# Peer weights of the first group loaded ahead, cache pages as four-key rows, and a new order inside a page group

## What is computed

```
xn = rmsnorm(x); q, c, kr, u_pool, gates = projections(xn @ w_in)
attn = prompt_attention(q, c, kr)                      # prompt: causal, 8 heads
# sample tokens: online softmax over 32 cached pages of 128 keys each, found by a page table
def page_step(carry, phys):
    m, l, acc = carry
    c_pg = ckv_pages[phys]; k_pg = mla_keys(c_pg, kr_pages[phys], p)
    s = einsum('bqhd,bthd->bhqt', q, k_pg) * SCALE
    return online_update(m, l, acc, s, c_pg)           # new maximum, exp, corrected sums
h = x + merge(attn, pool_mix(u_pool), gates) @ w_out
# PEER: per token and head, product keys pick 16 of 16384 experts
q = xn2 @ peer_w_q; s = q @ peer_keys; top 16 of 128 on each side, top 16 of the 256 sums
y = h + sum_e softmax_e * gelu(xn2 . peer_u[e]) * peer_v[e]
```

## Time and profile before

| | us |
|---|---|
| median of 3 runs | 3991.52 (3970.24 to 3993.34) |
| the profiled execution | 3977.99 |
| its span in the trace | 3976.2 |
| group 0 up to its scores | 0 to 292 |
| its scores, until the first expert dot | 292 to 416 |
| experts with groups 1 and 2 | 416 to 1930 |
| experts with the pages | 1930 to 3210 |
| experts with the sample layer, and the rest of the experts | 3210 to 3976 |

### The profile page before, as it was taken

One profiled execution on the slowest core, in us unless ns is written; L12 is line 12 of the kernel. 1 busy time (PEld: TensorE's weight loads), 2 busy tenths in 40 slices (PEclk: granted clock), 3 DMA queues, 4 the chain that ended last, 5 costly groups with the idle time before them and its releaser, 6 DMA issues.

```text
span 3976.2 us, 44748 instructions
## 1 busy us (share of the span) xinstructions
PE 3064.3 (77%) x13299; PEld 1596.3 (40%) x13299; DVE 2684.1 (68%) x6876; ACT 957.7 (24%) x1893; POOL 2394.3 (60%) x2196
## 2 busy tenths in 40 slices
PE   8896888996787888876688888888888866663345
PEld 5665435443442544333344444444444434230001
DVE  2312987665578866666788888888878875656653
ACT  2200123111023320120245444443454411100000
POOL 0000565765676566675766676676667676677776
PEclk9798988997998889998899999899989976666668
DMA  4445798999999989999999999899989999999999
GB/s 132 101 154 186 265 372 326 412 408 373 379 401 388 339 338 411 403 402 373 376 370 331 360 376 358 319 386 362 369 331 365 363 402 414 379 397 383 379 396 376
DMA packets 432834, 1387.34 MB, mean 349 GB/s; under 512 B 60553, under 2 KB 118890, under 8 KB 428306
## 3 DMA queue, kind: packets, MB, share of 16 engines
q0 software_dynamic: 313344, 1140.99, 74.5%
q1 hardware_dynamic: 119250, 243.49, 17.4%
HBM read 1354.17 MB, written 30.11 MB: 348 GB/s over the span
## 4 chain that ended last, share of the span: by engine, by line
PE 31%; DVE 20%; POOL 16%; DMA 15%; issue 10%; DVEq 3%; ACT 3%; SPq 1%; ACTq 0%; POOLq 0%
POOL arena L1559 16%; DMA arena<-in_peer_v,arena 8%; PE ps L1622 6%; DVE arena L1667 6%; PE ps L1872 6%; DMA arena<-in_w_peer 3%; PE ps L713 2%; PE ps L979 2%; DMA arena<-in_peer_u,arena 2%; PE ps L922 2%; DVE arena L2026 2%; PE ps L944 2%; PE ps L1903 2%; PE ps L879 1%; PE ps L856 1%
## 5 line engine op out<-in xcount | busy, mean ns | idle before, releaser
L1667 DVE CUSTOM_DVE_ANT_0 arena<-arena 128x1024 f32<-128x1024 f32 x1088 | 1319.7, 1223 | 562.2 <-DMA arena<-in_peer_u,arena 534.8
L1559 POOL DMA_INDIRECT arena<-in_peer_v,arena x1088 | 1194.0, 1097 | 798.2 <-PE ps L1622 503.6
L1559 POOL DMA_INDIRECT arena<-in_peer_u,arena x1088 | 1198.8, 1102 | 756.3 <-DVEq L1497 385.8
L1622 PE MATMUL ps<-arena 128*32 128x512 f32 x4352 | 693.6, 726 | 446.7 <-DMA arena<-in_peer_v,arena 441.4
L1872 PE MATMUL ps<-arena 128*128 128x512 f32 x1056 | 537.8, 633 | 11.0 <-ACT arena L1965 7.4
L1622 PEld LDWEIGHTS ps<-arena 128*32 128x32 f32 x4352 | 145.4, 124 | 852.3 <-issue 846.1
L979 PE MATMUL ps<-arena 128*128 128x384 f32 (+1 forms) x768 | 248.3, 477 | 57.9 <-DMA arena<-in_w_peer 57.6
L1965 ACT ACTIVATE arena<-ps 128x512 f32<-128x512 f32 x264 | 157.9, 598 | 431.6 <-PE ps L1872 430.0
L1872 PEld LDWEIGHTS ps<-arena 128*128 128x128 f32 x1056 | 188.5, 199 | 172.1 <-issue 162.6
L922 PE MATMUL ps<-arena 128*128 128x384 f32 (+1 forms) x768 | 233.0, 459 | 1.4 <-ACT arena L1135 1.4
L2026 DVE TENSOR_REDUCE arena<-arena 128x8 f32<-128x512 f32 x264 | 180.5, 684 | 79.1 <-ACT arena L1965 66.9
(11 more groups left out here) (232 smaller groups left out, 3719.0 us busy)
## 6 DMA issues: line engine op xcount, KB each, us to landing
arena<-in_w_merge SPq DMA_DIRECT2D x32, 1536.0 KB, 9.3
arena<-in_w_peer SPq DMA_DIRECT2D x64, 576.0 KB, 7.0
arena<-in_cache SPq DMA_DIRECT2D x256, 144.0 KB
arena<-in_peer_u,arena POOLq DMA_INDIRECT x1088, 8.2
arena<-in_peer_v,arena POOLq DMA_INDIRECT x1088, 8.2
arena<-in_w_front SPq DMA_DIRECT2D x33, 512.0 KB, 6.7
arena<-in_w_out SPq DMA_DIRECT2D x24, 512.0 KB, 8.8
arena<-s_dram SPq DMA_DIRECT2D x68, 128.0 KB
```

The source lines that it names most:

```text
L1559: self.nc.gpsimd.indirect_dma_start(out=ring[:, slot, :], out_offset=None, in_=self.I[table], in_offset=bass.IndirectOffsetOnAxis(ap=self. ...
L1622: mm = self.nc.tensor.matmul(self.acc[32 * j:32 * j + 32, n, :], self.diag[:, (q0 + j) // 16 % DIAGS, (q0 + j) % 16, :], self.v_ring[:, (q ...
L1667: self.nc.vector.tensor_tensor_reduce(out=u, in0=u, in1=self.xrep[jg % self.XBUF], scale=1.0, scalar=0.0, op0=ALU.mult, op1=ALU.add, accum ...
```

## The change

1. **Group 0's `w_peer` items get 16 places of their own** (in the space of the expert rings and what lies behind, unused as yet), and are loaded during the merge: three items behind each `w_merge` load of d = 2 to 6, the last behind d = 7. The first score step waits for all of them, the others for none; groups 1 and 2 keep the ring of three. The exponentials of the first `find` calls come one step later and behind the query copy.
2. **Cache pages as four-key rows.** The host puts the column of ones into the cache and shapes a page as 32 rows of 4 keys (4 x 289 values, 4624 bytes). Page j of a group goes to partitions j, j+4, j+8, ...; POOL no longer writes the ones.
3. **Order inside a page group.** PE's weighed sum of the group before moves from the head of the group to behind the keys of page 1; DVE's accumulation, SP's next page loads follow it by two slots; PE's spread of the maximum moves from before the keys of page 3 to behind them; ACT's root comes before the copy of page 0.

```diff
+    def p_item(self, g, j):
+
+        if not g.first:
+            return self.p_ring(j % 3)
+        word = self.ex.u_at + 9 * P * j if j < 7 else self.ex.spare + 9 * P * (j - 7)
+        return self.ar.at(word, P, 9, P)
...
             sp.dma_start(self.m_ring(d % 2), I["w_merge"][d]).then_inc(self.m_in[d % 2], 16)
+            if g.first:
+                for j in range(3 * d - 6, min(3 * d - 3, 2 * H)):
+                    self.load_peer(sp, g, j)
...
-                for j in range(2):
+                for j in range(0 if g.first else 2):
                     self.load_peer(sp, g, j)
-        self.load_peer(sp, g, 2)
+        if not g.first:
+            self.load_peer(sp, g, 2)
...
-                if j < 2 * H:
+                if j < 2 * H and not g.first:
...
-            pe.wait_ge(self.p_in[j % 3], 16 * ((6, 5, 5)[j % 3] * i + j // 3 + 1))
+            if not g.first:
+                pe.wait_ge(self.p_in[j % 3], 16 * ((6, 5, 5)[j % 3] * i + j // 3 + 1))
+            elif j == 0:
+                for r in range(3):
+                    pe.wait_ge(self.p_in[r], 16 * (6, 5, 5)[r])
...
-            if g.first and j >= 10 and j % 2 == 0:
-                self.rt.softmax(main.to(0), j // 2 - 5)
             act = main.to(g.after(f"s{j}") - 1)
             act.wait_ge(self.q_done, n + 1)
             if j >= 2:
                 act.wait_ge(self.k_done, n - 1)
             s.activation(self.qb(g, j % 2), ps[:, 2 + j % 2, 0:T], ACT.Copy).then_inc(self.q_out, 1)
+            if g.first and j >= 11 and j % 2:
+                self.rt.softmax(main.to(0), j // 2 - 5)
...
-            sp.dma_start(self.pages[par][:, j, 1:PGW], self.I["cache"][ds(page, 1)].rearrange("a p c -> (a p) c")).then_inc(self.page_in[par], 16)
+            sp.dma_start(self.pages[par][j:P:GP].rearrange("p a c -> p (a c)"),
+                         self.I["cache"][ds(page, 1)].rearrange("a p c -> (a p) c")).then_inc(self.page_in[par], 16)
...
-            sp = main.to(slot + PAGE_SLOTS + 1)
+            sp = main.to(slot + PAGE_SLOTS + 3)
...
-            if gi >= 2:
-                self.weigh(pe, self.group(gi - 2)[3], gi - 2, (gi - 2) % 3)
...
+                if gi >= 2 and j == 1:
+                    self.weigh(pe, self.group(gi - 2)[3], gi - 2, (gi - 2) % 3)
+                if 1 <= gi <= last and j == 3:
                     self.spread_maxima(pe, gi - 1)
-                if b and g == 1 and j == 2:
+                if b and g == 1 and j == 3:
...
+            if 1 <= gi <= last:
+                self.root(act, self.group(gi - 1)[3], gi - 1)
             if gi < last:
                 self.copy_page(act, 0, at, par)
-            if 1 <= gi <= last:
-                self.root(act, self.group(gi - 1)[3], gi - 1)
...
-            if gi >= 2:
-                self.accumulate(dve, gi - 2)
-                if self.group(gi - 2)[3] > GP:
-                    self.divide(dve, self.group(gi - 2)[0])
             for j in range(5):
                 dve = main.to(slot + 2 + j)
+                if gi >= 2 and j == 1:
+                    self.accumulate(dve, gi - 2)
+                    if self.group(gi - 2)[3] > GP:
+                        self.divide(dve, self.group(gi - 2)[0])
```

More of the change, by code:

```diff
@@ L591, in load_merge @@
         sp = main.to(g.after(f"a{last - 2}"))
+        if g.first:
+            sp.wait_ge(self.out_stored, self.outs_need(g))
         sp.wait_ge(self.s_done, g.unit0 + last + 1)
@@ L639, in load_peer @@
     def load_peer(self, sp, g, j):
-        sp.dma_start(self.p_ring(j % 3), self.I["w_peer"][j]).then_inc(self.p_in[j % 3], 16)
+        sp.dma_start(self.p_item(g, j), self.I["w_peer"][j]).then_inc(self.p_in[j % 3], 16)
     def keep_scores(self, main, g):
@@ L964, in keys @@
             for q in range(g.tiles):
-                last = t.matmul(ps[:, 4 + j % 2, q * P:(q + 1) * P], self.qb(g, j % 2)[:, q * P:(q + 1) * P], self.p_ring(j % 3)[:, 8, :],
+                last = t.matmul(ps[:, 4 + j % 2, q * P:(q + 1) * P], self.qb(g, j % 2)[:, q * P:(q + 1) * P], self.p_item(g, j)[:, 8, :],
                                 start=True, stop=True)
@@ L975, in pe_scores @@
                 pe.wait_ge(self.q_out, n - 1)
-            pe.wait_ge(self.p_in[j % 3], 16 * ((6, 5, 5)[j % 3] * i + j // 3 + 1))
+            if not g.first:
[3 more added lines that the diff above has]
+                    pe.wait_ge(self.p_in[r], 16 * (6, 5, 5)[r])
             for k in range(KD):
                 pe = main.to(g.at(f"s{j}", k / (KD + 1)))
-                last = t.matmul(ps[:, 2 + j % 2, 0:T], self.p_ring(j % 3)[:, k, :], xn2T[:, k, :], start=k == 0, stop=k == KD - 1)
+                last = t.matmul(ps[:, 2 + j % 2, 0:T], self.p_item(g, j)[:, k, :], xn2T[:, k, :], start=k == 0, stop=k == KD - 1)
             last.then_inc(self.q_done, 1)
@@ L1519, in __init__ @@
         self.xt = take(D)
+        self.u_at = w
         self.u_ring = take(RING, D)
@@ L1525, in __init__ @@
         self.a, self.a2, self.th, self.wt = take(2, 16), take(16), take(16), take(16)
+        assert self.spare + 9 * 9 * P <= w
         self.end = w
@@ L1842, in clear @@
             g.memset(self.qropes[s], 0.0)
-        for par in range(3):
-            for j in range(GP):
-                g.memset(self.pages[par][:, j, 0:1], 1.0)
         g.drain().then_inc(self.zeroed, 1)
@@ L1939, in tensor @@
                     self.keys(pe, j, n, at, gi, b)
-                if 1 <= gi <= last and j == 2:
+                if gi >= 2 and j == 1:
+                    self.weigh(pe, self.group(gi - 2)[3], gi - 2, (gi - 2) % 3)
+                if 1 <= gi <= last and j == 3:
                     self.spread_maxima(pe, gi - 1)
-                if b and g == 1 and j == 2:
+                if b and g == 1 and j == 3:
                     self.result(pe, b - 1)
@@ L2006, in scalar @@
                     self.copy_page(act, j + 1, at, par)
-                if b and g == 1 and j == 3:
+                if b and g == 1 and j == 4:
                     self.copy_result(act, b - 1)
@@ L2375 @@
     peer_w = np.stack([np.concatenate([chunked(A["peer_w_q"][0][:, j * P:(j + 1) * P]), keys[j][:, None, :]], axis=1) for j in range(2 * H)])
+    cache = np.concatenate([np.ones((NPHYS, PAGE, 1), np.float32), A["cache_ckv"][0], A["cache_krope"][0]], axis=2)
     arrays = {
@@ L2382 @@
         "stateT": A["state_pool"][0].reshape(DB, STATE, G, P).transpose(3, 2, 0, 1),
-        "page_table": A["page_table"].reshape(1, DB * NPAGES), "cache": np.concatenate([A["cache_ckv"][0], A["cache_krope"][0]], axis=2),
+        "page_table": A["page_table"].reshape(1, DB * NPAGES), "cache": cache.reshape(NPHYS, PAGE // GP, GP * PGW),
         "w_merge": merge_w, "w_out": chunked(A["w_out"][0]), "norm2": np.tile(A["norm2_w"], (P, 1)), "w_peer": peer_w,
```

## The result

The changed kernel takes **4036.91 us** (median of 4 runs, 4015.84 to 4047.85); the kernel before, run beside it, 3980.89 us (4 runs, 3970.24 to 3993.34). The ratio is 1.0125, 95% interval 1.0097 to 1.0154: **slower** by 1.25%, clear of the noise, and outside the forecast's range (3905 to 4010 us). The profiled execution took 4029.57 us, 4027.8 us of it span. (A ratio is that of its own comparison, with its 95% interval in brackets from here on; it can differ from the quotient of the two medians by up to 0.2%.)

A forecast was written before the change was run, and what follows sets the result against it. The pages' stretch was taken as DVE and PE taking turns, DMA close behind. Terms -33 - 0 - 27 + 0 + 26 + 7 + 10 = -17 gave 3961 us; forecast median 3965 us, range 3905 to 4010.

The forecast's parts named there:

- Part 1: Preload, group 0's scores: `find` calls and first expert dot earlier, dot at about 383 us; -33 us, or -28.
- the preload does not pay: Rival, group 0's scores: finds stay bound by the scores' loads, merge 14 us longer; -5 instead of -33, 3993 us; chance 0.06.
- Part 2: Four-key rows, page loads: same bytes in a quarter of the packets; 0 us, other end 12 us saved.
- the second rival: Pages' stretch: late pages, PE's first transposes wait for a load, slower than before; 4033 us; chance 0.14.
- Part 3: New order inside a page group, pages' stretch: terms -27, 0, +26, +7, +10; stretch 1280 + 16 us.
- For PE that is even: 0, with -14 and +40 as ends.: PE, root ahead of copies: 109 us of new standing against 122 us of vanishing waits (exponentials, copies, spread).
- Root ahead, -27: ACT's root ahead of the copy of page 0: DVE's 26.7 us of waits for roots go; -27 us.
- spread, +7: Spread behind the last keys: DVE's subtraction waits about 0.5 us in a fifth of cases; +7, ends 0 and 32.
- Pages two slots later, +10: SP's later page loads: room of 7.3 us mostly covers issue and landing; +10 us, ends 0 and 220.
- Weighed sum behind the keys, +26: DVE's accumulation waits 1.95 us for the sum in a fifth of groups; +26 us, ends 0 and 125.
- The first rival: Pages' stretch gets shorter: half of DVE's 90 us of waits go, nothing replaces them; 3905 us; chance 0.27.

The follow-up runs named there:

- the sum put back: Changed kernel with weighed sum at the group's head, accumulation and page loads at their old places, root and spread as changed: 3968.11 us, 0.9951.
- A: Runs on the kind of chip where the kernel before takes 3981 to 3988 us; they bear the argument.
- B: Runs on the kind of chip where the kernel before takes 4126 to 4153 us; not used for prices.
- early pages: Changed kernel whose page loads do not wait for the weighed sum (sums read a constant array, attention's result left out): 4026.98 us, 1.0098; on slower chips 1.0383.
- the two remedies at once: Changed kernel with page loads one group early (constant array in the sums) and accumulation one slot later; only on slower chips: 1.0227 and 1.026.
- the version behind the keys of page 0: Changed kernel with weighed sum behind page 0's keys, loads one slot sooner, root behind the copies, accumulation behind the new maximum: 3955.49 us, 0.9935.

## Why the prediction was wrong, step by step

- **Part 1, right.** Forecast -33 us with the first dot at 383; measured 380.64, and 33 us by the medians (38 by the ratio) in the run that keeps it, with the rows. The merge is 1 us longer, where the prediction took nothing and 14 us at worst. Its rival, that the preload does not pay, is out.
- **Part 2, not contradicted.** Forecast 0, other end -12. Packet time of SP's queue: 11.2% of 1280 us before is 143 us, 10.5% of 1305 us with the sum put back is 137: 6 us, unfelt, since DVE does not wait for gathers (2.7 us there). On A no run prices the rows alone; on B they may cost 0.5%. That 32 partitions at a time would be slow, the case of the second rival, does not show: the new order with 128 partitions in a load is as slow, and PE waits as long for its pages. (The Trainium skill, "SBUF — State Buffer", section "Summary: rules for kernel authors", says to use 128 partitions for a DMA-bound transfer; for these page loads no run here shows a gain from it.) SP's issue of one did grow, 0.48 us for 0.34.
- **Part 3, wrong.** Forecast -27 + 0 + 26 + 7 + 10 = +16 us; the order costs 1.0125 - 0.9905 = 2.2%, 88 us. The terms:
  - *"For PE that is even: 0, with -14 and +40 as ends." **This is the step that failed.*** The prediction set 109 us of new standing behind ACT's copies against 122 us of waits that vanish. The 101 us for exponentials and for the spread did vanish. But in the run with early pages, where no page is late, the wait for copies is 146.7 us, the wait for maxima grows from 39.5 to 65.8 and that for squares from 7 to 24, and PE's idle time in the stretch goes from 183 us to 259: +76, where 0 was written. The fault is in the balance: a wait for exponentials at the group's head is not saved by moving the sum. PE is waiting on the chain that also makes the copies, and the wait reappears at whatever PE does next in that place. The runs of A show it: exponentials 93.7, or pages 118.1 with exponentials 16.3, or copies 146.7, or copies 99.2.
  - *Root ahead, -27, and spread, +7.* Root and spread together cost 0.46%, 18 us (13 by the medians), in intervals that barely overlap, instead of giving 20. DVE's wait for roots fell from 27 to 10 us as forecast, and no time came of it.
  - *Pages two slots later, +10, measured +41 with the sum at the head and +13 with the sum late.* Here the size was off. The landing was estimated at 4.7 us from one quarter of an item, where it is 4.0 to 6.4 in the chain; the way from the sum's end to the last issue was taken as the 3.64 us of issuing, where it is 4.5. In the group shown that is 10.8 us against a room of 7.3. The room itself was read well: 3.5 us late by that sum, 2.92 bare. The prediction named the sign (a wait on the cache) and the bound, 4.7 us, from which this rival decides, and then took its own estimate at the very bound. The price of a microsecond was wrong the other way: 64 us for each, where 1.8 us a group (118.1 / 64) cost 41, since two thirds stood in place of the wait for exponentials.
  - *Weighed sum behind the keys, +26, measured +30 beside late pages and +59 without them, and by another way.* The sum of 26 was DVE standing 1.95 us in a fifth of the groups. DVE stood 104 us in 50 groups, and taking that away gave nothing in the changed kernel. That the cost lies in the sum's place on PE is what is left, not what a run shows. That the sum no longer fills PE's gap at the head cannot be all of it: behind the keys of page 0 it does not fill it either, and that version is 0.3% behind the old order, in intervals that overlap. Whether it is the sum standing ahead of the keys of pages 2 and 3, or what follows the sum one page later, stays open.
- **The rivals.** The second, late pages, slower, had 0.14 and 4033 us; 4037 came. The direction and the sign in the profile are its own, but its mechanism carries 41 of the 88 us by one order of adding the parts and 13 by the other; that the number fits is in part chance. The first rival, half of DVE's waits gone and 3905 us, is refuted: DVE's waits for squares and roots fell from 90 to 50 us, 104 us for the sum came in their place, and PE's idle time grew by 78 us.

Open: root and spread apart, the sum one page later or earlier by itself, and the two remedies at once on A.

## What to carry to other kernels

Where engines take turns in a ring, cost a move by the ring's length, not by the waits that it clears: ask what the engine does instead of that wait, and if the answer is "waits for the next link", write 0. A buffer's release moved later has to be timed link by link (end of the reader, all issues before the last one, landing under this load), and where the room that is left equals your estimate of the landing, that is an even chance and not a small term. The longest wait in a profile is worth what a run without it gives: here 104 us were worth 0, 107 us some 13 (not clear of the noise), and 118 us 41. So add up all the idle time of an engine before and after, and not only the wait that went.

## What the runs showed that was not expected

- The same kernel takes 3.5 to 4.3% longer on some chips (3981 to 3988 against 4126 to 4153 us), more than half of it in the pages' stretch: preload and rows take 1381 us there and 1312 on A, 69 of the 112 us between their spans (4069.9 and 3958.2). ACT stops for up to 14.8 us at a time in it without a releaser. Why is open.
- The same change can have another price on them: early page loads -0.3% on A, inside the intervals, and +1.7% on B, outside them.
- One page's difference in where PE's weighed sum stands, with the loads that follow it, goes with some 1.5% of the whole time (the version behind the keys of page 0 against the changed kernel, root and accumulation taken off).
- A page load of four-key rows (144.5 KB, 32 partitions) takes SP 0.48 us to issue where 128 rows take 0.34, for a quarter of the packets.
